# A two-layer hybrid decoder trunk: full-height GLA level products, and copies, squares, a gate product and row sends on other engines

## The reference

```
h = x @ w_in                                   # 256 x 3088
A: 4 heads, a = softmax(q1 k1) - lam * softmax(q2 k2);  oa = rms_norm(a @ v) * (1 - lam_init)
B: 6 heads, dilated windows (128,1), (512,4), (2048,16), combined by their denominators
C: 4 heads, gated linear attention (GLA), key width 48, value width 96:
   scores[i,j] = sum_d q[i,d] k[j,d] exp(b[i,d] - b[j,d])  for j <= i,  b = cumsum(log decay)
   oc = rms_norm(scores @ v) * gla_g * silu(gate)
out = concat(oa, ob, oc) @ w_out
```

## Time and profile before

| | |
|---|---|
| median of 3 runs | 1691.65 (1691.62 to 1691.7) |
| the profiled execution | 1691.62 |
| its span, first to last instruction | 1689.8 |
| TensorE busy | 1665.7, 99% |
| VectorE busy | 1352.9, 80% |
| ScalarE busy | 1046.3, 62% |
| GpSimd busy | 25.6, 2% |
| mean granted TensorE clock | 0.997 of full |
| memory read | 286 GB/s with what is written, over the span |

### The profile page before, as it was taken

How to read it: one execution, slowest core, us unless ns; L and a number is a source line. 1 busy time by engine, 2 the same in 40 slices (tenths; PEclk the granted TensorE clock), 3 DMA queues, 4 the chain that set the end, 5 groups by cost and what they waited for, 6 DMA issues and landing times.

```text
span 1689.8 us, 22174 instructions
## 1 busy us (share of the span) xinstructions
PE 1665.7 (99%) x8238; PEld 1377.9 (82%) x8238; DVE 1352.9 (80%) x1252; ACT 1046.3 (62%) x927; POOL 25.6 (2%) x33
## 2 busy tenths in 40 slices
PE   9999999999999999999999999999999999999996
PEld 7888888888888888878888888888888888888885
DVE  4787756545667885799898898898998998998997
ACT  4565344334346634377777777777777777777774
POOL 0000000000000000011000000000000000000000
PEclk9999999999999999999999999999999999999998
DMA  8523446446455544699999999999999999999992
GB/s 298 170 104 131 159 134 212 162 151 226 163 199 214 186 171 154 210 348 404 393 386 379 351 385 369 357 383 367 366 380 366 361 378 362 372 377 354 380 373 93
DMA packets 211002, 478.63 MB, mean 283 GB/s; under 512 B 14496, under 2 KB 17344, under 8 KB 210752
## 3 DMA queue, kind: packets, MB, share of 16 engines
q1 hardware_dynamic: 209952, 475.69, 77.8%
q0 software_dynamic: 576, 2.10, 0.3%
q10 hardware_dynamic: 416, 0.04, 0.0%
HBM read 474.65 MB, written 9.44 MB: 286 GB/s over the span
## 4 chain that ended last, share of the span: by engine, by line
PE 91%; DVE 5%; DMA 1%; ACT 1%; issue 1%; DVEq 0%; SPq 0%; ACTq 0%
PE ps L2342 51%; PE ps L1777 22%; PE ps L2197 4%; PE ps L1820 3%; DVE w_lo L1101 2%; PE ps L1816 2%; PE ps L2324 1%; PE ps L1737 1%; PE ps L2036 1%; PE ps L2117 1%; PE ps L2098 1%; PE ps L1972 1%; DVE late L1241 1%; DMA ring<-in_xa_wkv_dram 1%; DMA ring<-in_w_in_dram 0%
## 5 line engine op out<-in xcount | busy, mean ns | idle before, releaser
L1101 DVE TENSOR_TENSOR w_lo<-ring,w_hi 128x2048 fp32r<-128x2048 f32 x336 | 766.3, 2289 | 88.8 <-ACT w_hi L753 86.7
L753 ACT CAST w_hi<-ring 128x2048 fp32r<-128x2048 f32 x336 | 641.2, 1910 | 243.1 <-PE ps L2342 241.1
L2342 PE MATMUL ps<-w_hi,xe_hi 128*128 128x512 f32 x896 | 243.7, 394 | 0.2 <-DVE xe_lo L1584 0.2
L2342 PE MATMUL ps<-w_lo,xe_hi 128*128 128x512 f32 x896 | 240.4, 390 | 2.3 <-DVE w_lo L1101 2.3
L2342 PE MATMUL ps<-w_hi,xe_lo 128*128 128x512 f32 x896 | 239.9, 390 | 0.0
L2342 PEld LDWEIGHTS ps<-w_lo,xe_hi 128*128 128x128 f32 x896 | 167.7, 188 | 39.2 <-DVE w_lo L1101 4.6
L2342 PEld LDWEIGHTS ps<-w_hi,xe_lo 128*128 128x128 f32 x896 | 168.2, 188 | 35.8
L1777 PE MATMUL ps<-ring_r,xT_r 128*128 128x512 f32 (+1 forms) x736 | 194.3, 392 | 1.7 <-ACT ring_r L720 1.0
L2342 PEld LDWEIGHTS ps<-w_hi,xe_hi 128*128 128x128 f32 x896 | 165.2, 188 | 32.3 <-DVE xe_lo L1584 0.3
L1777 PEld LDWEIGHTS ps<-ring_r,xT_r 128*128 128x128 f32 x736 | 135.1, 188 | 33.6 <-DVE late_r L1085 1.6
L2342 PE MATMUL ps<-w_hi,he_hi 128*128 128x512 f32 x448 | 141.7, 397 | 0.0
(11 more groups left out here) (317 smaller groups left out, 1906.2 us busy)
## 6 DMA issues: line engine op xcount, KB each, us to landing
ring<-in_moe_w_dram SPq DMA_DIRECT2D x336, 1024.0 KB, 6.1
ring<-in_ffd_w_dram SPq DMA_DIRECT2D x31, 1024.0 KB, 5.1
ring<-in_w_in_dram SPq DMA_DIRECT2D x23, 1024.0 KB, 5.8
ring<-in_xa_wkv_dram SPq DMA_DIRECT2D x16, 1024.0 KB, 5.1
ring<-in_w_out_dram SPq DMA_DIRECT2D x8, 1024.0 KB, 5.1
ring<-in_xa_wq_dram SPq DMA_DIRECT2D x8, 1024.0 KB, 5.3
ring<-in_xa_wo_dram SPq DMA_DIRECT2D x8, 1024.0 KB, 5.1
sent_rows<-in_zeros_dram SPq DMA_DIRECT2D x12, 512.0 KB, 7.1
```

Source lines behind the costliest of these rows:

```text
L753: act.copy(w_hi[:, q % SPLIT_SLOTS, :], ring[:, RAW_ORDER[q % RAW_SLOTS], :]).then_inc(hi_ready, 1)
L1101: dve.tensor_tensor(w_lo[:, q % SPLIT_SLOTS, :], ring[:, RAW_ORDER[q % RAW_SLOTS], :], w_hi[:, q % SPLIT_SLOTS, :].bitcast(F32), ALU.subtr ...
L2342: ins = pe.matmul(ps[:, bank, :], xs[:, k, :], w[:, c, cols], start=(first and m == 0), stop=(last and m == 2))
```

## The change

1. Steps 1 to 7 of the GLA are multiplied over all 128 partitions at once. The decayed queries of the two heads are written into separate column ranges of `qk`, with zeros on the other head's partitions, so that 4 products of 128 rows and 128 columns take the place of 8 of 64 rows and 64 columns. Both heads' results lie in one PSUM bank. `products` writes the queries with two instructions, one for each head's 64 partitions; `combine` makes one predicated copy of 512 elements instead of two of 256; the tile `st` has its axes swapped; `clear` clears both halves of a buffer.
2. Pieces 1 and 3 are taken by VectorE, at its units 3 and 6. The chunks of pieces 6 and 7 behind steps 7 and 8 are dealt out anew.
3. The copy of the differential output and its square move from ScalarE to VectorE, the copy behind the level exponents of unit 4. The decay exponentials are one instruction in ScalarE's unit 5.
4. In `difference` the reciprocal sums are multiplied by lambda first, in an instruction of 128 x 2, and the scaling then has one factor instead of two.
5. The gate's product with `gla_norm_g` moves from VectorE to GpSimd, behind `clear(0)`.
6. The sends no longer wait for splits, and the sorted rows are loaded behind half 24 instead of half 34.

```diff
-                    if first and q == 34:
+                    if first and q == 24:
                         sp.wait_ge(rows_out, 16 * 2 * T)
                         load_rows(1)
...
-                pool.memset(qk[:, parity, 1, :], 0.0).then_inc(zeros_ready, 1)
+                pool.memset(qk[:, parity, :, :], 0.0).then_inc(zeros_ready, 1)
...
-                        pool.wait_ge(lo_ready, SENT_AT[2 * t + c])
...
+                pool.wait_ge(gate_silu, l + 1)
+                for t in range(T):
+                    gate = h[:, t, C_G:C_RANK].rearrange("p (h k) -> p h k", h=CH)
+                    pool.tensor_tensor(gate, gate, g_c[:, l, :].unsqueeze(1).to_broadcast([P, CH, CV]), ALU.mult)\
+                        .then_inc(gate_scaled, 1)
...
-                    if u == 4:
-                        act.wait_ge(pv_done, UNITS * l + 4)
-                        act.copy(o_tok[:, :, 0:S], ps[:, 0, :].rearrange("p (t n) -> p t n", t=T)).then_inc(oa_taken, 1)
...
-                    for i in ((0,), (), (), (1,), (2,), (3,), (4,))[u]:
-                        take_piece(l, i)
-                    if u == 4:
+                    if u in (0, 4, 6):
+                        take_piece(l, (0, None, None, None, 2, None, 4)[u])
+                    if u == 5:
                         act.wait_ge(dec_diff, l + 1)
-                        act.wait_ge(oa_taken, l + 1)
-                        act.activation(oa_sq, o_tok[:, :, 0:S], ACT.Square).then_inc(oa_squared, 1)
-                        act.activation(dec[:, 0:4, :], dec[:, 0:4, :], ACT.Exp, scale=-1.0)
-                    if u == 5:
-                        act.activation(dec[:, 4:8, :], dec[:, 4:8, :], ACT.Exp, scale=-1.0).then_inc(dec_exp, 1)
+                        act.activation(dec, dec, ACT.Exp, scale=-1.0).then_inc(dec_exp, 1)
...
+            def take_piece(l, i):
+                dve.wait_ge(kv_psum, 2 * KV_P * l + i + 1)
+                dve.tensor_copy(piece_out(i), ps[:, piece_bank(i), :]).then_inc(kv_dve, 1)
...
+                    done(dve.tensor_scalar(rs[:, 1::2], rs[:, 1::2], lams[:, 3:4], None, ALU.mult))
...
-                                                rs[:, 2 * j + 1:2 * j + 2], lams[:, 3:4], ALU.mult, ALU.mult)
+                                                rs[:, 2 * j + 1:2 * j + 2], None, ALU.mult)
...
                     if u == 3:
+                        take_piece(l, 1)
                         split_low(1)
                     if u == 4:
                         for v in range(2, LEVELS):
                             level_exponents(v)
                         cross_exponents()
                         dve.sem_inc(dec_diff, 1)
+                    if u == 6:
+                        take_piece(l, 3)
+                    if u == 4:
+                        dve.wait_ge(pv_done, UNITS * l + 4)
+                        done(dve.tensor_copy(o_tok[:, :, 0:S], ps[:, 0, :].rearrange("p (t n) -> p t n", t=T)))
+                        dve.sem_inc(oa_taken, 1)
                     if u == 5:
-                        dve.wait_ge(oa_squared, l + 1)
+                        done(dve.tensor_tensor(oa_sq, o_tok[:, :, 0:S], o_tok[:, :, 0:S], ALU.mult))
...
+                    if s <= LEVELS:
+                        into = qk[:, s % 2, 0, :].rearrange("p (b h n i) -> p b h n i", b=4, h=2, i=half)
+                        for hp in range(2):
+                            r = slice(64 * hp, 64 * hp + 64)
+                            q4, d4 = (v[r, :, upper].rearrange("p (b n) i -> p b n i", b=4) for v in (qs, ds))
+                            dve.tensor_tensor(into[r, :, hp], q4, d4, ALU.mult)
...
-                        for hp in range(2):
-                            into = st[:, hp].rearrange("p b (n w) -> p b n w", n=n)[:, :, :, half:]
-                            src = ps[:, level_bank(s, hp), 0:S].rearrange("p (b n i) -> p b n i", b=4, n=n)
-                            ins = dve.copy_predicated(into, mask, src)
+                        into = st.rearrange("p b h (n w) -> p (b h) n w", n=n)[:, :, :, half:]
+                        mask = level[:, s - 1, :].rearrange("p (n i) -> p n i", n=n).unsqueeze(1).to_broadcast([P, 8, n, half])
+                        ins = dve.copy_predicated(into, mask,
+                                                  ps[:, level_bank(s), :].rearrange("p (m n i) -> p m n i", m=8, n=n))
...
                     if u == 4:
                         pe.wait_ge(oa_taken, l + 1)
-                        pe.wait_ge(kv_act, KV_ACT * l + 2)
+                        pe.wait_ge(kv_dve, KV_DVE * l + 1)
...
-                            for hp in range(2):
-                                r = slice(64 * hp, 64 * hp + 64)
-                                ins = pe.matmul(ps[:, level_bank(s, hp), up], qk[r, s % 2, 1, at], qk[r, s % 2, 0, up],
-                                                start=True, stop=True)
+                            at = slice(b * P, (b + 1) * P)
+                            ins = pe.matmul(ps[:, level_bank(s), at], qk[:, s % 2, 1, at], qk[:, s % 2, 0, at],
+                                            start=True, stop=True)
...
                     elif s == 7:
-                        piece(l, 6, range(4, 5))
+                        piece(l, 6, range(4, 6))
                     else:
-                        piece(l, 6, range(5, 8))
+                        piece(l, 6, range(6, 8))
+                        piece(l, 7, range(0, 1))
...
-                piece(l, 7, range(0, 5))
+                piece(l, 7, range(1, 6))
...
-                piece(l, 7, range(5, 8))
+                piece(l, 7, range(6, 8))
```

More of the change, by code:

```diff
@@ L121 @@
 EXTRAS_AT = [8, 11, 15, 19, 23]
-SENT_AT = [13, 17, 21, 25]
 LEVELS = 7
@@ L270, in bass_decoder @@
         spare = ring[:, RAW_SLOTS - 1, :]
-        st = spare[:, 0:8 * P].rearrange("p (h b s) -> p h b s", b=4, h=2)
+        st = spare[:, 0:8 * P].rearrange("p (b h s) -> p b h s", b=4, h=2)
         stx = spare[:, 8 * P:12 * P].rearrange("p (b h s) -> p b h s", b=2, h=2)
@@ L328, in bass_decoder @@
         kv_psum = sem("kv_psum")
-        kv_act = sem("kv_act")
+        kv_act, kv_dve = sem("kv_act"), sem("kv_dve")
         q_act, q_dve = sem("q_act"), sem("q_dve")
@@ L351, in bass_decoder @@
         gla_out, gla_square = sem("gla_out"), sem("gla_square")
-        oa_squared = sem("oa_squared")
+        gate_scaled = sem("gate_scaled")
         mixed = sem("mixed")
@@ L388, in bass_decoder @@
         POWERS = 3 + 3 * T
-        KV_ACT = 8
+        KV_ACT, KV_DVE = 6, 2
         TURN = {"x0": 0, "mem": 1}
@@ L483, in wait_used, with level_bank @@
                 engine.wait_ge(acc_ready[2 * (u % 2) + 1], u // 2 + 1)
-        def level_bank(s, hp):
-            return (5 if s % 2 else 4) + 2 * hp
+        def level_bank(s):
+            return 5 if s % 2 else 7
         def cross_bank(t, i):
@@ L1330, in products @@
                         dve.wait_ge(level_scores, GSTEPS * l + s - 1)
-                    dve.tensor_tensor(qk[:, s % 2, 0, 0:S].rearrange("p (m i) -> p m i", i=half), qs[:, :, upper],
-                                      ds[:, :, upper], ALU.mult)
+                    if s <= LEVELS:
[4 more added lines that the diff above has]
+                            dve.tensor_tensor(into[r, :, hp], q4, d4, ALU.mult)
+                    else:
+                        dve.tensor_tensor(qk[:, s % 2, 0, 0:S].rearrange("p (m i) -> p m i", i=half), qs[:, :, upper],
+                                          ds[:, :, upper], ALU.mult)
                     dve.tensor_tensor(qk[:, s % 2, 1, :].rearrange("p (m w) -> p m w", w=2 * half)[:, :, lower],
@@ L1341, in combine @@
                             src = ps[:, 4 + 2 * hp, :].rearrange("p (b q) -> p b q", b=4)
-                            ins = dve.tensor_tensor(st[:, hp], src, ident.unsqueeze(1).to_broadcast([P, 4, P]), ALU.mult)
+                            ins = dve.tensor_tensor(st[:, :, hp], src, ident.unsqueeze(1).to_broadcast([P, 4, P]), ALU.mult)
                     else:
@@ L1345, in combine @@
                         n = P // (2 * half)
-                        mask = level[:, s - 1, :].rearrange("p (n i) -> p n i", n=n).unsqueeze(1).to_broadcast([P, 4, n, half])
-                        for hp in range(2):
-                            into = st[:, hp].rearrange("p b (n w) -> p b n w", n=n)[:, :, :, half:]
-                            src = ps[:, level_bank(s, hp), 0:S].rearrange("p (b n i) -> p b n i", b=4, n=n)
-                            ins = dve.copy_predicated(into, mask, src)
+                        into = st.rearrange("p b h (n w) -> p (b h) n w", n=n)[:, :, :, half:]
+                        mask = level[:, s - 1, :].rearrange("p (n i) -> p n i", n=n).unsqueeze(1).to_broadcast([P, 8, n, half])
+                        ins = dve.copy_predicated(into, mask,
+                                                  ps[:, level_bank(s), :].rearrange("p (m n i) -> p m n i", m=8, n=n))
                     done(ins)
@@ L1365, in _ @@
```

(19 more changed lines are left out.)

1 line of the change is left out of this document (removed).

## The result

The changed kernel took 1701.24 (median of 5, 1698.8 to 1701.54) where the kernel before took 1691.62 (median of 5, 1691.25 to 1691.7): a ratio of 1.0053, 95% interval 1.0038 to 1.0067. The forecast was 1690.0 with a range up to 1693.5, and "slower by over 0.2%" had a chance of 0.08. The profiled execution took 1701.23, 9.61 more than that of before, with a span of 1699.4.

What follows compares the result with a forecast made beforehand. The prediction took TensorE, busy for 99% of the span, as the bound. Per layer +1.47 - 2.25 = -0.8, twice -1.6, gave 1690.0 from 1691.62; its own range was 1689.0 to 1691.2, with rivals B, C and E 1687.9 to 1693.5.

Steps and rivals of the forecast that it cites:

- part 6: Gate product on GpSimd: nothing won on VectorE, clearing hidden, GpSimd gives way to VectorE; taken as 0.
- part 2: GLA levels on VectorE: 1.85 a level, so VectorE becomes the pace, with 0.84 of waits a layer.
- Part 4: Attention units: differences make TensorE 0.24 late, VectorE's late copy leaves it 1.2 idle; costs 1.47 per layer.
- Part 1: GLA levels on TensorE: a level with its piece falls from 1.94 to 1.58.
- Rival E: GLA levels on TensorE: a level stays at 1.04 + 0.90, only Part 3 is kept; 1693.3, chance 0.13.
- rival B: GLA levels: VectorE does not become the pace, its products or copy being cheaper; 1688.3, chance 0.12.
- Part 3: Before the GLA output: TensorE's wait on ScalarE and the restart go, 0.65 together per layer.
- Part 5: ScalarE's decay exponentials become one instruction of 3.6; the delay of unit 6's copies stays just hidden, cover 0.2.
- rival C: GpSimd's gate product holds VectorE out while it runs; 1691.4, or 1693 to 1695, chance 0.15.
- Part 7: Sends of routed rows: four start at 736.6, done by 747, no wait on queue SP; taken as 0.
- Rival D: Sends of routed rows: the four wait for each other's landing; +3.0, 1693.0, chance 0.07.

Runs made afterwards that it cites:

- experiment 1: The changed kernel with the copy of the differential output back on ScalarE: 1695.24 against 1701.24.
- 2: The changed kernel with the gate product back on VectorE: 1697.42 against 1701.24.
- 10: The whole changed kernel with 112 wait instructions on a reached semaphore put into TensorE's list: 1698.69 against 1701.24.
- experiment 12: The kernel of experiment 9 with one of the two half-height products of a level left out (output incomplete): 1685.51.
- experiment 9: The changed kernel with the differential output's copy, gate product and difference as before, plus 112 wait instructions in TensorE's list: 1689.87.
- experiment 7: The kernel before with only the chunks of key/value pieces 6 and 7 dealt out anew: 1690.05, ratio 0.9991.
- experiment 6: The kernel before with only the sends not waiting for splits and the sorted rows loaded behind half 24: 1691.74.
- 11: The kernel before with 145 wait instructions on a reached semaphore put into TensorE's list: 1692.88, ratio 1.0008.
- experiment 3: The changed kernel with six float32 products that nobody reads ahead of TensorE's wait before unit 4's values: 1699.12 against 1701.24.

## Why the prediction was wrong, step by step

The forecast of 1690.0 was 11.2 short. Two of its terms failed: the gate product on GpSimd, put at 0, cost 1.50 and 1.57 (part 6), and VectorE as the pace of the levels, put at 0.84 a layer, cost 2.11 and 2.10 (part 2), together 5.6. Part 4's copy and difference were 1.1 short. The load (1.19) and the clock (1.54 and 1.15) had no term at all.

The terms a layer, in us, as forecast and as measured:

| term | forecast | layer 0 | layer 1 | read from |
|---|---|---|---|---|
| difference | +0.24 | +0.42 | +0.46 | experiment 1 |
| copy of the differential output | +1.23 | +1.54 | +1.59 | 1 and 2; in layer 1, 1 and 10 |
| levels and chunks without a wait for VectorE | -3.09 | -3.05 | -3.04 | 12 |
| VectorE as the pace of the levels | +0.84 | +2.11 | +2.10 | 12 and 9 |
| gate product on GpSimd | 0 | +1.50 | +1.57 | 2 |
| clock | - | +1.54 | +1.15 | the changed kernel and 2; in layer 1, it and 10 |
| rest | | -0.01 | +0.26 | |
| sum | -0.78 | +4.05 | +4.09 | |

With the load (+1.19) and the start (+0.33, scatter) that is 9.66.

**Part 1 was right.** A level was forecast at 0.86 and 0.72 on TensorE, 1.58 together; experiment 12 shows 0.89 and 0.70. Rival E, a level that stays at 1.04, is out. The Trainium skill's advice to pack 64 contraction rows in two tiles (TensorEngine Tiling (Array Packing), section When to Use Tiling) does not hold here for TensorE's time: experiment 12's 0.89 stands against the 1.04.

**Part 2 was right in the mechanism and wrong in the size: this step lost 1.27 of the forecast gain in layer 0 and 1.26 in layer 1.** VectorE became the pace (rival B is out), at 2.08 instead of 1.85. The failed term is "three products at 0.34 start to start = 1.01". They take 145.95 - 144.74 = 1.21, because the second half-height product starts only 0.43 behind the first, and the key product 0.44 behind that. Between rows of before that overlap it is 0.34, and in experiment 12, where all of them start at partition 0, it is 0.34 again. The Trainium skill has this (VectorE: DVE Perf Modes, section Two Vector instructions with no wait between them): an instruction whose operands start in another group of 32 partitions than those of the one ahead "starts only when every earlier Vector instruction has finished". The trace agrees; 0.43 + 0.44 + 0.34 is the 1.21, and the prediction did not reckon with it. The copy was 0.87 with what lies behind it (0.69 + 0.15 = 0.84 forecast). Then each wait costs more than itself: the level behind one takes 1.13 in the changed kernel's chain, where it takes 0.89 without:

```profile
157.37 1.13 PE ps L2050 x8
```

The forecast's 0.84 was three waits, before levels 5 to 7, without a slower start. In TensorE's timeline of experiment 9, where the gate product does not disturb, there are four. Those before levels 4 and 5 are

```profile
143.84 1.13 PE L2052 MATMUL ps<-qk 128*128 128x128 f32 x8 [0.25 <-DVEq L1363]
...
148.12 1.13 PE L2052 MATMUL ps<-qk 128*128 128x128 f32 x8 [0.36 <-DVEq L1363]
```

and 0.24 and 0.23 stand before levels 6 and 7, 1.08 together. Level 3 too has the length of 1.13 there, where the first two have 1.05. The other 1.03 of the 2.11 is the slower start of these five levels. So the 0.23 a level became 1.27 a layer.

**Part 3 was right**: 0.65 forecast, 0.67 measured in either layer (experiment 7). It is the one part of the change that wins alone, and it does most of what the change wins in the GLA.

**Part 4 was right in kind and 0.5 short.** The idle was forecast at 1.2 and was 1.35; the values behind it start 0.24 slower, which was not in the sum. The tiny instruction was taken at 0.18, the price of a reciprocal of 128 x 4, and the cheaper scaling at 0.35; VectorE's groups by form in the changed kernel, 90 to 122 us (busy, mean ns), have

```profile
L1266 DVE TENSOR_SCALAR late<-late,rsum 128x256 f32<-128x256 f32 x4 | 1.2, 350 | 0.1
...
L1266 DVE TENSOR_SCALAR late<-late,rsum 128x128 f32<-128x128 f32 x4 | 1.0, 284 | 0.1
L1263 DVE TENSOR_SCALAR rsum<-rsum,lams 128x2 f32<-128x2 f32 x4 | 0.9, 228 | 0.1
```

0.35 was right and 0.228 is not 0.18. Half of the scalings have 128 columns, which the prediction did not say, but they save as much: 346 to 284, against 410 to 350. In the kernel before they are

```profile
L1264 DVE TENSOR_SCALAR late<-late,rsum,lams 128x128 f32<-128x128 f32 x4 | 1.2, 346 | 0.1
```

By the two chains a difference became 0.14 to 0.15 longer from the end of its reciprocal, instead of 0.08; three of them are the 0.42.

**Part 5 was right.** The one exponential, on ScalarE's timeline of the changed kernel, took

```profile
131.00 3.62 ACT L841 ACTIVATE late<-late 128x4096 f32<-128x4096 f32 x1
```

and TensorE did not wait for ScalarE's copies behind it: the last one for unit 6 ended at 137.31 and the values started at 137.65, 0.34 of cover where 0.2 was forecast.

**Part 6 was wrong: rival C is what happened.** The argument was that VectorE lost nothing beside an indirect send and 0.06 beside a power. But neither was what the change adds, a GpSimd product of 384 elements beside VectorE products of two tensors. Here VectorE's product began 0.02 behind GpSimd's and took 1.27, the next one 1.14, where one takes 0.42 alone. Rival C's own prices, 1691.4 and 1693 to 1695 against 1690.0, are 0.7 and 1.5 to 2.5 a layer (its working for both products at 1.65 gives 3.3 - 0.3 = 3.0 and 1696.0); it was 1.50 and 1.57. The Trainium skill's SBUF — State Buffer, section SBUF: two separate sides, calls this an exclusive lock that goes to the one that starts first. This pair agrees. The power and the split beside it do not, in the changed kernel as little as in the one before: GpSimd's power starts at 127.76 for 1.65, the split 0.01 behind it, and it takes 2.34 instead of 2.28. What sets the two pairs apart is open.

**Part 7 was right.** The sends were forecast from 736.6 to 747. In experiment 6, which isn't late by then, they run from 737.35 to 744.76; in the changed kernel they start at 747.02 and end at 754.4 (GpSimd's timeline, first and last of four):

```profile
747.02 2.32 POOL L651 DMA_INDIRECT sent_rows<-x,row_i  x1 [36.14 <-DVE row_i L1668]
...
753.48 0.95 POOL L651 DMA_INDIRECT sent_rows<-x,row_i  x1 [0.30 <-issue]
```

SyncE waited for VectorE's splits alone between 730 and 800. Rival D is out.

**Missing altogether** were the instruction fetch in layer 1's load (+1.19; that its place decides is shown by experiments 9 to 11) and the clock. At layer 1's start it fell in five of the seven traces whose load was late and in none of the seven with a load of 8.9 to 9.1. Of the 5.91 between the load's landing and those first transposes TensorE is busy for 3.55 in the changed kernel, whose row by stretch follows, and for 4.74 in the kernel before:

```profile
525.60:531.51 5.91, 3.55 (x27) 3.04 (x26) 3.74 (x4) 3.57 (x4) 0.00 (x0) 0.99 1.12 439
```

Behind the idle before unit 4's values it fell in layer 0 in two of the four traces that have that idle (changed, 10), in layer 1 in none, and in layer 0 in none of the ten traces without the idle. What decides between the two, with the same idle ahead, is open; experiment 3 doesn't tell. A clock that falls in some executions alone would also account for the changed kernel's runs lying 2.7 us apart, where those of before lie within 0.5. Layer 1's rest of 0.26 (experiments 2 and 9) is open as well.

The best complete version is experiment 9: new levels, chunks and sends with the list's length kept, 1689.87, 0.1% under the kernel before. Experiment 7, four lines of the change, cannot be told from it: 1690.05.

## What to carry to other kernels

When work moves onto the engine that is second on the path, price it by its start-to-start time in the very form it will have: which partition each instruction starts at, what GpSimd runs beside it, and what the waiting engine pays at the start behind a wait. Where two engines are close in pace, an error of 0.2 us a step is multiplied by the number of steps and comes on top of a slower start behind each wait. And when a part of the program that nobody touched gets slower, look at the instruction queue: adding or removing instructions moves its fetches, and a transfer that the path waits for may now share its time with one. A few instructions that do nothing, placed early, tell this apart; reckon with their own price (0.3 here).

## What the hardware showed that was not expected

- One instruction fetch of 16 KB inside a 1 MB weight load that was waited for delayed it by 1.2 us: 10.0 to 10.2 in seven traces with the fetch inside, 8.9 to 9.1 in seven without.
- 112 or 145 waits on a reached semaphore, put between matmuls of 512 columns, cost 0.3: the 28 matmuls took 7.08 to 7.11 in four traces with them and 6.77 to 6.79 in ten without.
- A VectorE product of 256 elements is followed after 0.34 by one that starts at the same partition, after 0.43 or 0.44 by one that starts at another.
- GpSimd's product of 128 x 384 tripled VectorE's product of 256 elements that started 0.02 behind it (1.27 against 0.42); its power of 128 x 8 cost a split that started 0.01 behind it 0.06 (2.34 against 2.28).
